# A hybrid trunk on one core: the 256-column fp32r matmuls read their moving operand as two interleaved halves

## The reference

```
for l in range(DEPTH):                                   # DEPTH = 2
    x = x + token_mixer(rmsnorm(x, ln1_g[l]), w_in[l], ...)
    h = rmsnorm(x, ln2_g[l])
    x = x + swiglu(h, ...)        if l % 2 == 0          # dense, D_FF = 2816
    x = x + moe(h, w_router, ...) if l % 2 == 1          # top 2 of 8 experts, D_FF_EXPERT = 3584
return rmsnorm(x, final_g)
```

## Time and profile before

| | |
|---|---|
| runs | 1519.89, 1521.44, 1521.6 us |
| profiled execution, first to last instruction (span) | 1517.2 us |
| median of the runs less that span | 4.2 us |
| PE busy | 1486.0 us, 98% |
| PE weight loads busy | 1088.7 us, 72% |
| DVE, ACT, POOL busy | 473.7, 338.0, 99.6 us |
| granted TensorE clock, mean | 0.993 |

### The profile page before, as it was taken

How to read it: one execution, slowest core, us unless ns; L and a number is a source line. 1 busy time by engine, 2 the same in 40 slices (tenths; PEclk the granted TensorE clock), 3 DMA queues, 4 the chain that set the end, 5 groups by cost and what they waited for, 6 DMA issues and landing times.

```text
span 1517.2 us, 48076 instructions
## 1 busy us (share of the span) xinstructions
PE 1486.0 (98%) x21630; PEld 1088.7 (72%) x21630; DVE 473.7 (31%) x840; ACT 338.0 (22%) x478; POOL 99.6 (7%) x128
## 2 busy tenths in 40 slices
PE   8999999999999998999999999999999999999996
PEld 7999989999899985666666666666666666666664
DVE  6674765445667464200200200200200200200202
ACT  5554454444555432001001001001001001001001
POOL 0551000000055000000000000000000000000000
PEclk9999999999999999999999999999999999999998
DMA  9754545556555473999999999999999999999991
GB/s 321 256 167 168 166 145 188 188 174 205 162 185 167 140 292 107 375 397 389 378 395 388 384 395 381 394 390 379 395 397 381 388 398 383 384 398 386 386 391 69
DMA packets 186545, 456.41 MB, mean 301 GB/s; under 512 B 13760, under 2 KB 79584, under 8 KB 186336
## 3 DMA queue, kind: packets, MB, share of 16 engines
q1 hardware_dynamic: 186336, 453.35, 80.1%
HBM read 452.26 MB, written 1.05 MB: 299 GB/s over the span
## 4 chain that ended last, share of the span: by engine, by line
PE 96%; DVE 1%; ACT 1%; issue 0%; DMA 0%; POOL 0%; SPq 0%; POOLq 0%; DVEq 0%
PE bank L1201 95%; DMA gain<-in_ln_dram 0%; PE bank L1616 0%; PE bank L1318 0%; POOL rs L1142 0%; DVE mem L701 0%; ACT mem L488 0%; DVE xt_lo L722 0%; ACT w_hi L465 0%; ACT xt_hi L494 0%; DVE x L730 0%; DVE w_lo L668 0%; PE bank L1347 0%; PE bank L1295 0%; PE bank L1234 0%
## 5 line engine op out<-in xcount | busy, mean ns | idle before, releaser
L1201 PE MATMUL bank<-mem 128*32 128x256 f32 (+1 forms) x16240 | 883.3, 378 | 0.8 <-DVE mem L1055 0.6
L1201 PEld LDWEIGHTS bank<-mem 128*32 128x32 f32 (+1 forms) x16240 | 529.1, 110 | 348.2 <-issue 1.3
L668 DVE TENSOR_TENSOR w_lo<-mem,w_hi 128x1024 fp32r<-128x1024 f32 x182 | 227.0, 1258 | 173.8 <-ACT w_hi L465 173.3
L1201 PE MATMUL bank<-xt_hi,w_hi 128*128 128x256 f32 x880 | 249.5, 284 | 3.5 <-DVE w_lo L668 2.7
L1201 PE MATMUL bank<-xt_lo,w_hi 128*128 128x256 f32 x880 | 248.8, 283 | 0.0
L1201 PE MATMUL bank<-xt_hi,w_lo 128*128 128x256 f32 x880 | 248.6, 282 | 0.0
L465 ACT CAST w_hi<-mem 128x1024 fp32r<-128x1024 f32 x182 | 189.6, 1050 | 218.2 <-PE bank L1201 213.2
L1201 PEld LDWEIGHTS bank<-xt_hi,w_hi 128*128 128x128 f32 x880 | 166.8, 190 | 6.4 <-issue 4.3
L1201 PEld LDWEIGHTS bank<-xt_lo,w_hi 128*128 128x128 f32 x880 | 165.7, 188 | 0.4
L1201 PEld LDWEIGHTS bank<-xt_hi,w_lo 128*128 128x128 f32 x880 | 165.9, 189 | 0.0
L1100 DVE TENSOR_TENSOR mem<-mem,bank 128x512 f32<-128x512 f32 x24 | 16.5, 688 | 396.0 <-PE bank L1201 396.0
(11 more groups left out here) (174 smaller groups left out, 872.5 us busy)
## 6 DMA issues: line engine op xcount, KB each, us to landing
mem<-in_eg_dram SPq DMA_DIRECT2D x224, 512.0 KB, 6.5
mem<-in_eu_dram SPq DMA_DIRECT2D x224, 512.0 KB, 7.1
mem<-in_ed_dram SPq DMA_DIRECT2D x224, 512.0 KB, 6.9
mem<-in_w_in_dram SPq DMA_DIRECT2D x42, 1024.0 KB, 5.4
mem<-in_fg_dram SPq DMA_DIRECT2D x11, 1024.0 KB, 5.1
mem<-in_fu_dram SPq DMA_DIRECT2D x11, 1024.0 KB, 5.3
mem<-in_fd_dram SPq DMA_DIRECT2D x11, 1024.0 KB, 4.9
mem<-in_w_br_dram SPq DMA_DIRECT2D x8, 1024.0 KB, 5.0
```

Of the source, the lines that this page charges most:

```text
L668: nc.vector.tensor_tensor(w_lo[:, q % H, :], src, w_hi[:, q % H, :].bitcast(F32), ALU.subtract).then_inc(lo_done, 1)
L1201: return nc.tensor.matmul(out, lhs, rhs, start=first, stop=last, skip_group_check=True)
```

## The change

`turns` rearranges a moving operand of 256 columns so that it is read 0, 128, 1, 129, and so on; column n of the result therefore holds token (or weight column) n/2 of the first half if n is even, of the second half if it is odd. `unturned` is the view of a bank that undoes this: it reads every second column of a 256-column block, first the even ones, then the odd ones. `halves` gives the destination the same three dimensions, and `own` picks the columns of one token block out of an operand that was left in the turned order. No instruction is added, removed or moved on any engine, and every one keeps its size; only addresses differ.

```diff
+        def turns(ap, parts=2):
+            return ap.rearrange("p (b a) -> p a b", b=parts)
+        def unturned(ap, blocks=1):
+            return ap.rearrange("p (m a b) -> p m b a", m=blocks, b=2)
+        def own(ap, t):
+            return ap.rearrange("p (a b) -> p a b", b=TB)[:, :, t]
+        def halves(ap):
+            return ap.rearrange("p m (b a) -> p m b a", b=2)
...
-                nc.scalar.mul(qT[:, :, :], src[:, :].rearrange("p (b t) -> p b t", b=HP), DK ** -0.5).then_inc(q_done, 1)
+                nc.scalar.mul(halves(qT[:, :, :]), unturned(src[:, :], HP), DK ** -0.5).then_inc(q_done, 1)
...
-                    nc.vector.tensor_tensor(u[:, 2 * n:2 * n + 2, 2:SEQ + 2], src[:, :].rearrange("p (b t) -> p b t", b=2),
-                                            cv[:, 2 * n:2 * n + 2, :], ALU.mult).then_inc(gc_done, 1)
+                    nc.vector.tensor_tensor(halves(u[:, 2 * n:2 * n + 2, 2:SEQ + 2]), unturned(src[:, :], 2),
+                                            halves(cv[:, 2 * n:2 * n + 2, :]), ALU.mult).then_inc(gc_done, 1)
...
@@ channels @@
-                                      (xt_hi[:, kk, :], xt_lo[:, kk, :]),
+                                      (turns(xt_hi[:, kk, :]), turns(xt_lo[:, kk, :])),
@@ tokens @@
-                                      pair(w, lambda a: a[:, k, :]), kk == 0 and t == 0, kk == KT - 1 and t == TB - 1)
+                                      pair(w, lambda a: turns(a[:, k, :])), kk == 0 and t == 0, kk == KT - 1 and t == TB - 1)
@@ branch @@
-                                          (y[0][:, kk, :], y[1][:, kk, :]), kk == 0 and b % 2 == 0,
+                                          (turns(y[0][:, kk, :]), turns(y[1][:, kk, :])), kk == 0 and b % 2 == 0,
@@ down_part @@
-                                   (fh_hi[:, s, k, t * P:(t + 1) * P], fh_lo[:, s, k, t * P:(t + 1) * P]),
+                                   (own(fh_hi[:, s, k, :], t), own(fh_lo[:, s, k, :], t)),
@@ router @@
-                ins = mm3(bank[0][0:NE, 0:SEQ], (wr_hi[:, k, :], wr_lo[:, k, :]), (xt_hi[:, k, :], xt_lo[:, k, :]),
+                ins = mm3(bank[0][0:NE, 0:SEQ], (wr_hi[:, k, :], wr_lo[:, k, :]),
+                          (turns(xt_hi[:, k, :]), turns(xt_lo[:, k, :])),
```

More of the change, by code:

```diff
@@ L513, in _ @@
                 src = full(l, "q")
-                nc.scalar.mul(qT[:, :, :], src[:, :].rearrange("p (b t) -> p b t", b=HP), DK ** -0.5).then_inc(q_done, 1)
+                nc.scalar.mul(halves(qT[:, :, :]), unturned(src[:, :], HP), DK ** -0.5).then_inc(q_done, 1)
                 after(2)
                 src = full(l, "k")
-                nc.scalar.copy(kT[:, :, :], src[:, :].rearrange("p (b t) -> p b t", b=HP)).then_inc(k_done, 1)
+                nc.scalar.copy(halves(kT[:, :, :]), unturned(src[:, :], HP)).then_inc(k_done, 1)
                 act.wait_ge(abs_done, l + 1)
@@ L524, in _ @@
                     src = full(l, f"v{n}")
-                    nc.scalar.copy(v[:, :, 256 * n:256 * n + 256],
-                                   src[:, :].rearrange("p (b n) -> p b n", b=TB)).then_inc(v_done, 1)
+                    nc.scalar.copy(halves(v[:, :, 256 * n:256 * n + 256]), unturned(src[:, :], TB)).then_inc(v_done, 1)
                 act.wait_ge(b_done, l + 1)
@@ L532, in _ @@
                     src = full(l, f"xc{n}")
-                    nc.scalar.copy(cv[:, 2 * n:2 * n + 2, :],
-                                   src[:, :].rearrange("p (b t) -> p b t", b=2)).then_inc(xc_done, 1)
+                    nc.scalar.copy(halves(cv[:, 2 * n:2 * n + 2, :]), unturned(src[:, :], 2)).then_inc(xc_done, 1)
                 for h in range(HP):
@@ L545, in _ @@
                     src = full(l, f"go{n}")
-                    nc.scalar.activation(gs[:, :, 256 * n:256 * n + 256],
-                                         src[:, :].rearrange("p (b n) -> p b n", b=TB), ACT.Silu).then_inc(silu_done, 1)
+                    nc.scalar.activation(halves(gs[:, :, 256 * n:256 * n + 256]), unturned(src[:, :], TB), ACT.Silu
+                                         ).then_inc(silu_done, 1)
                 for n in range(8):
@@ L556, in _ @@
                     src = full(l, name)
-                    nc.scalar.activation(gate[:, n // 4, 2 * (n % 4):2 * (n % 4) + 2, :],
-                                         src[:, :].rearrange("p (b t) -> p b t", b=2), ACT.Sigmoid).then_inc(gate_done, 1)
+                    nc.scalar.activation(halves(gate[:, n // 4, 2 * (n % 4):2 * (n % 4) + 2, :]),
+                                         unturned(src[:, :], 2), ACT.Sigmoid).then_inc(gate_done, 1)
                 for t in range(TB):
@@ L759, in _ @@
                 src = full(l, "alow")
-                nc.vector.tensor_copy(al[0:RANK, :], src[0:RANK, 0:SEQ]).then_inc(al_done, 1)
+                nc.vector.tensor_copy(al[0:RANK, :].rearrange("p (b a) -> p b a", b=2),
+                                      unturned(src[0:RANK, 0:SEQ])[:, 0, :, :]).then_inc(al_done, 1)
                 after(0)
@@ L829, in _ @@
                     src = full(l, f"gb{n}")
-                    nc.vector.tensor_tensor(cv[:, 2 * n:2 * n + 2, :], src[:, :].rearrange("p (b t) -> p b t", b=2),
-                                            cv[:, 2 * n:2 * n + 2, :], ALU.mult).then_inc(ya_made, 1)
+                    turned_cv = halves(cv[:, 2 * n:2 * n + 2, :])
+                    nc.vector.tensor_tensor(turned_cv, unturned(src[:, :], 2), turned_cv, ALU.mult).then_inc(ya_made, 1)
                 after(11)
@@ L877, in branch_a @@
                         dve.wait_ge(gate_done, 8 * l + 2 * n + m + 1)
-                        nc.vector.tensor_tensor(gate[:, 0, kk:kk + 2, :], gate[:, 0, kk:kk + 2, :],
-                                                src[:, :].rearrange("p (b t) -> p b t", b=2), ALU.mult).then_inc(pa_done, 1)
+                        half_gate = halves(gate[:, 0, kk:kk + 2, :])
+                        nc.vector.tensor_tensor(half_gate, half_gate, unturned(src[:, :], 2), ALU.mult).then_inc(pa_done, 1)
                 after(21)
@@ L895, in _ @@
                         dve.wait_ge(gate_done, 8 * l + 4 + 2 * n + m + 1)
-                        nc.vector.tensor_tensor(gate[:, 1, kk:kk + 2, :], gate[:, 1, kk:kk + 2, :],
-                                                src[:, :].rearrange("p (b t) -> p b t", b=2), ALU.mult).then_inc(pb_done, 1)
+                        half_gate = halves(gate[:, 1, kk:kk + 2, :])
+                        nc.vector.tensor_tensor(half_gate, half_gate, unturned(src[:, :], 2), ALU.mult).then_inc(pb_done, 1)
                     until(base + 2 * (23 + n) + 1 + H)
@@ L974, in _ @@
             dve.wait_ge(lg_full, 1)
-            nc.vector.tensor_copy(lt, bank[0][0:NE, 0:SEQ]).then_inc(lt_done, 1)
+            nc.vector.tensor_copy(lt.rearrange("p (b a) -> p b a", b=2), unturned(bank[0][0:NE, 0:SEQ])[:, 0, :, :]
+                                  ).then_inc(lt_done, 1)
             dve.wait_ge(lg_full, 2)
```

## The result

The changed kernel takes 1494.85 us (median of four runs, 1492.81 to 1496.81) against 1521.51 us of the kernel before (four runs, 1519.89 to 1521.6). The ratio is 0.9829, its 95% interval 0.9815 to 0.9843: 26.7 us less, well clear of the spread of the runs, though under 2% of the time. The forecast was 1491 us in a range of 1477 to 1532.

The account below looks back on a forecast made before the run. PE, busy in 98% of the span, was taken as the bound. Faster turned matmuls took 30.1 us off the 1517.2 us span, other terms 0, giving 1487.1; with 4.2 us for the median, 1491.3 us, range 1477 to 1532.

Parts of the forecast that it names:

- What bounds: Mixers and dense part: PE alone bounds, so what a matmul gains from start to start enters the time in full.
- Price of one: Each turned matmul in mixers, dense part and router takes 110.9 ns, 9.1 or 6.4 ns less; 30.1 us in sum.
- the chance of 0.56: Chance given to a gain, from 3 ns per turned matmul to the whole excess: 1477 to 1511 us.
- The excess is in the moving stream: Turned matmuls: the 13.3 ns over 106.7 in `channels`, about 11 in `tokens`, come mostly from reading the moving operand.
- Half rate, the rival: Every turned matmul loses a cycle per element: 98 ns more each, 336 us, so 1857 us; chance 0.20.
- Weight loads of `down_part`: Loads with a step of two, even if 101 ns longer, stay hidden beside 512-column matmuls: 0 us.
- Reads of the banks: ACT and DVE undoing the order with a stride of two: taken as 0, 1.1 us if the per-column part doubled.
- Who is late next: In a 5.3 us unit DVE's work takes 3.2 us, ACT's less; nothing new becomes the bound.

Follow-up runs that it names:

- run 2: Changed kernel, but dense-part gate and up products alternate between halves after two neighbours in one kind of step, after four in the other; 1533.81 us, single run.
- run 3: Changed kernel, but dense-part gate and up products stream with a plain step of 16 bytes in one kind of step, 8 bytes in the other; 1625.07 us, single run.
- run 6: Changed kernel, but dense-part gate and up products take turns among four quarters, or alternate between two runs of 64 bytes; 1514.72 us, single run.
- run 4: Changed kernel with the bank-seeding zeros read as 256 neighbours and the router's keep-warm zeros read in the turned order; 1496.21 us, single run.
- run 1: Changed kernel with the 512-column matmuls of out_piece and down_part turned too, residual additions reading banks with a stride of two; 1486.5 us, ratio 0.9772 to before.
- run 7: Kernel before with only the dense part's gate and up products turned, down reading its stationary operand with a step of two; 1512.29 us, ratio 0.9946.

## Why the prediction was right

*What bounds.* Right: the stretches of nothing but PE took up nearly the whole gain. By the means of the distances in the two traces (120.0 to 111.7 for `channels` and `branch`, 117.3 to 111.7 for `tokens`, 116.8 to 109.0 in the router) it is 3024 x 8.3 + 384 x 5.6 + 24 x 7.8 ns = 25.1 + 2.2 + 0.2 = 27.4 us, and the span fell by 26.3. Of the 1.1 us between them 0.7 is DVE's lateness (below); the rest was not separated (gaps between units, and the clock at the start of each layer, below).

*Price of one.* The direction was right and the size a little off: 110.9 ns expected, 112 measured (108.9 in the router), and so 30.1 us expected where 26.7 came. The term came from matmuls that read one address again and again. Per 256 columns they take 108.8 ns, and I added the whole 4.2 ns over 512 columns to 106.7; 256 columns in turns with a full weight load take 3 ns more. I had called the term a choice, and it was: nothing in the trace of before said that alternating would relieve the stream rather than hurt it, so the direction was in part luck, as the chance of 0.56 says. Runs 2, 3 and 6 show how near the other answer was. Of the nine orders that ran besides plain neighbours, five were slower than neighbours: hops of four by 7 ns, quarters by 27, hops of two and both steps by 50 to 113.

*The excess is in the moving stream.* Right, and now shown for the part that went: it goes with the order of reading, and with nothing else changed (all of `channels`); it is there with zeros as data and with overwriting matmuls (run 4); with 512 columns it is two to three times as large (18 ns, run 1, against 8.3 in `channels` and 5.6 in `tokens`). It does not need a full weight load (8 ns in the router with 8 stationary columns in the kernel before, 5 by the rows of run 7; 8 ns in `channels` with 128). Why it is 5.6 ns in `tokens` and 8.3 in `channels`, with the same shapes, no run shows.

*Half rate, the rival.* It fell for this order, and yet the price I gave it was about right where it does occur: 110 to 113 ns for a plain step of 8 or 16 bytes (run 3), against the 98 of my estimate. The Trainium skill ("Advanced Engine Details and Errata", section SBUF Cachelines) asks for at least two hits on a 16-byte line and has a different line for each access as slow. The 16-byte step agrees with it (233 ns). The changed kernel doesn't: each access is in another line than the last, and no order is faster. Nor does the 8-byte step, which has two hits per line and is at 230 ns. Applied to every second element of the stream the rule fits seven of the ten orders; hops of two, quarters and, by a few ns, hops of four stay outside.

*Weight loads of `down_part`.* At 0, right: 196 ns for 188, hidden. *Reads of the banks.* At 0, right: 595 and 680 ns.

*Who is late next.* "Nothing new becomes the bound" was nearly right. PE's largest wait for DVE's splits of weights is 2.1 us and stands once, as before. New is the wait in front of `out_piece` for DVE's `xt_lo` (line 925 of the kernel after), once per layer: the matmuls of `branch` got faster, DVE's work between them and `out_piece` did not. It costs 0.35 us each time, 0.7 us of the gain.

*A reading that was wrong.* The prediction held against the half rate that the scores, with a step of two elements, have a median of 219 ns. That is a modelled duration, not a distance of starts. By the starts in the trace of before a set of four scores takes 58 ns, with 32 columns and with 64 alike, so something other than the columns sets it, and even at half rate 32 columns (27 ns at 2.4 GHz) would not show. Nor are the scores the only moving operands that are not contiguous: `wide_unit` reads runs of 32 columns that lie 128 apart (`strided`), as fast as `expert_down` reads 256 neighbours (216 ns per set of four by the starts), but its matmuls are plain fp32 with four column tiles at a time.

*The start.* The profiled execution of after does not begin better than that of before: both reach the second unit at 26.6 to 26.8 us, although 72 turned matmuls lie ahead. The stretches of both kernels (busy us of PE, PEld, DVE, ACT, POOL; then the granted clock) show why, before:

```profile
12.00:15.60 3.60, 1.65 (x8) 1.25 (x6) 2.72 (x5) 3.19 (x6) 0.00 (x0) 0.73 1.12 327
15.60:19.40 3.80, 3.01 (x23) 2.83 (x24) 3.80 (x6) 3.68 (x5) 0.00 (x0) 1.00 1.09 331
```

and after:

```profile
12.00:15.60 3.60, 1.54 (x8) 1.14 (x6) 2.72 (x5) 3.30 (x6) 0.00 (x0) 0.50 1.12 322
15.60:19.40 3.80, 3.73 (x17) 3.76 (x18) 3.80 (x5) 3.75 (x5) 0.00 (x0) 0.50 1.09 332
```

In the one the clock is back at 2.4 GHz by 15.6 us, in the other it is at 1.2 GHz up to 19.4: 17 matmuls for 23. It comes after the same idle stretch for the first normalisation in both. Run 7, whose mixers are those of the kernel before, has most of it too:

```profile
15.60:19.40 3.80, 3.42 (x17) 3.29 (x18) 3.80 (x6) 3.80 (x5) 0.00 (x0) 0.62 1.09 326
```

So such a start does not need the change. In the second layer it is the other way round: there the first 72 matmuls begin at 1.2 GHz in the kernel before and at 2.4 GHz in the kernel after, and take 9.77 and 8.28 us. I take both for chance; one profiled execution of each kernel can't show more.

**What stays open.** Why an order with hops of two takes 170 ns, and quarters 147, where two turns would have both near the 230 of the plain steps: in these two a way comes back to a line after one other (four elements of it in the quarters, two in the hops), in the steps never soon. A way might keep more than one line; no run separates that. Whether there are two ways at all is open too, and so is what sets the size of the neighbours' excess, which differs between `channels` and `tokens` and between two executions of the same router. Nor is it known where the 3 ns between 8 and 128 stationary columns come from: with 512 turned columns and a load of 128 the distance is 216.2 ns, only 2.9 over the 213.3 of the columns.

## What to carry to other kernels

Where fp32r matmuls of N columns start some 10% later than every N / 2.4 ns at the clock of 2.4 GHz, and PE is the bound, let the moving operand alternate between two runs that are contiguous in themselves (two halves, or runs of 16 bytes or more): 120 ns become 112 for 256 columns, 234 become 216 for 512, and ACT and DVE read the bank with a stride of two at no cost. Measure the order first, in the distance of starts: two elements per hop, four places in turn or a plain stride look alike on paper and cost 27 to 113 ns. Then look who is late next: here DVE was, before `out_piece`. Turn every fp32r stream, not the 256-column ones only: run 1 is the fastest kernel that its time can tell, 1486.5 us, 2.3% under before.

## What the runs showed of the hardware that I had not expected

Successive columns of an fp32r stream may come from different places at no cost, and even with a gain: 112 ns for 0, 4, 1, 5, 2, 6, 3, 7 and 120 for 0, 1, 2, 3. What is slow is a plain step: two elements or four halve the rate (230 and 233 ns), which nothing in the kernel before had shown, since its only step of two was in matmuls of 32 columns that other limits hold back (58 ns per set of four).

The costs of the orders do not scale with TensorE's clock. The step of 16 bytes takes 237 ns at 1.2 GHz and 233 at 2.4, and the 8 ns of the neighbours are nothing at 1.2 GHz, where both orders take 213 ns.
